# A modulation row stored earlier on VectorE, and the last unit's products and turns in another order, in a two-layer transformer with a Strassen-like MLP

## The reference, cut to what matters

```python
def squared_relu_mlp(h, w_up, w_down):                 # w_up 1024x4096, w_down 4096x1024
    return jnp.square(jax.nn.relu(h @ w_up)) @ w_down
for layer in range(2):
    h = h + mixer(rmsnorm(h, ...))                     # layer 0: recurrence + attention, layer 1: "cd"
    h = h + memory_cross_attention(rmsnorm(h, ...), mem, ...)
    h = h + squared_relu_mlp(rmsnorm(h, mlp_norm[layer]), mlp_w_up[layer], mlp_w_down[layer])
x = rmsnorm(h, final_norm)
mod = jax.nn.silu(c) @ w_ada + b_ada                   # 6 * 1024 numbers, for the second block
x = x + gate1 * hybrid_mixer(rmsnorm(x) * (1 + scale1) + shift1, ...)
x = x + gate2 * expert_choice_ffn(rmsnorm(x) * (1 + scale2) + shift2, ...)
```

## Time and profile before

| what | value |
| --- | --- |
| time, median of 3 runs | 1793.9 us (1791.47 to 1796.63) |
| time of the profiled execution | 1789.16 us |
| its span, first to last instruction | 1787.4 us |
| TensorE busy / weight loads busy | 1545.1 us (86%) / 1140.7 us (64%) |
| VectorE busy / ScalarE busy | 582.3 us (33%) / 260.1 us (15%) |
| mean granted TensorE clock | 0.936 of full speed |

### The profile page before, as it was taken

The page is one execution under the profiler, slowest core; times in us unless marked ns, Lnnn a source line. Parts: engine busy times, 40 slices in busy tenths (PEclk is TensorE's granted clock), DMA queues, the critical chain, the costliest instruction groups (busy, mean ns, idle before and its releaser), DMA issues.

```text
span 1787.4 us, 20576 instructions
## 1 busy us (share of the span) xinstructions
PE 1545.1 (86%) x8896; PEld 1140.7 (64%) x8896; DVE 582.3 (33%) x1259; ACT 260.1 (15%) x610; POOL 30.2 (2%) x52
## 2 busy tenths in 40 slices
PE   6999999999998999999899899989977666655665
PEld 4868688887876777788788788768863222121211
DVE  3633015355633420243556646642330000000000
ACT  1332021000011520210000222222020000000000
POOL 0000000000010000000000002000000000000000
PEclk9999999999999999999999899998979987888877
DMA  9325316664433054157644101432739999999997
GB/s 391 143 94 188 142 48 235 235 253 171 177 141 142 1 192 166 44 210 283 259 147 146 48 1 66 135 107 96 298 126 417 429 429 429 429 429 430 427 429 313
DMA packets 42826, 395.27 MB, mean 221 GB/s; under 512 B 15856, under 2 KB 18288, under 8 KB 19056
## 3 DMA queue, kind: packets, MB, share of 16 engines
q1 hardware_dynamic: 42032, 392.46, 55.4%
q0 software_dynamic: 272, 1.05, 0.2%
q10 hardware_dynamic: 432, 0.44, 0.1%
HBM read 391.31 MB, written 2.62 MB: 220 GB/s over the span
## 4 chain that ended last, share of the span: by engine, by line
PE 72%; DMA 22%; DVE 3%; issue 1%; ACT 1%; ACTq 0%; DVEq 0%
PE pb L445 53%; DMA ring<-in_w_experts 22%; PE pb L836 11%; PE pb L533 6%; DMA small_w<-in_small_w 1%; ACT arena L1315 1%; PE pb L594 1%; PE pb L654 0%; PE pb L1141 0%; DVE arena L1936 0%; DVE hT L1936 0%; DVE rstd L1668 0%; PE pb L1148 0%; PE pb L1001 0%; DVE xT L1915 0%
## 5 line engine op out<-in xcount | busy, mean ns | idle before, releaser
L445 PE MATMUL pb<-hT,ring 128*128 128x256 f32 x2176 | 484.2, 383 | 1.4 <-issue 1.4
L445 PEld LDWEIGHTS pb<-hT,ring 128*128 128x128 f32 x2176 | 413.0, 191 | 64.9 <-issue 9.7
L1315 ACT ACTIVATE arena<-pb 128x512 f32<-128x512 f32 (+4 forms) x166 | 77.9, 480 | 519.5 <-PE pb L445 427.6
L2286 DVE SCALAR_TENSOR_TENSOR side<-side,pb 128x256 f32<-128x256 f32 x16 | 6.7, 421 | 411.6 <-ACT side L1315 411.6
L445 PE MATMUL pb<-ring,hT 128*32 128x512 f32 (+2 forms) x512 | 91.3, 634 | 36.7 <-DMA ring<-in_w_experts 36.7
L533 PE MATMUL pb<-arena,ring 128*128 128x256 f32 x512 | 118.2, 382 | 0.0
L445 PE MATMUL pb<-arena 128*64 128x128 f32 (+5 forms) x592 | 90.4, 420 | 28.5 <-DMA arena<-in_w_experts 16.0
L445 PE MATMUL pb<-ring,arena 128*32 128x512 f32 (+1 forms) x416 | 68.3, 770 | 49.6 <-DMA ring<-in_w_experts 49.6
L533 PEld LDWEIGHTS pb<-arena,ring 128*128 128x128 f32 x512 | 94.9, 190 | 14.6 <-issue 2.9
L445 PEld LDWEIGHTS pb<-arena 128*64 128x64 f32 (+3 forms) x592 | 53.9, 159 | 62.8 <-issue 26.9
L445 PEld LDWEIGHTS pb<-ring,hT 128*32 128x32 f32 (+1 forms) x512 | 32.3, 139 | 84.7 <-DMA ring<-in_w_experts 45.3
(11 more groups left out here) (297 smaller groups left out, 1705.8 us busy)
## 6 DMA issues: line engine op xcount, KB each, us to landing
ring<-in_w_dense SPq DMA_DIRECT2D x86, 2048.0 KB, 8.2
ring<-in_w_experts SPq DMA_DIRECT2D x72, 2048.0 KB, 36.3
arena<-in_w_experts SPq DMA_DIRECT2D x24, 2048.0 KB, 35.9
ring<-in_w_dense SPq DMA_DIRECT2D x2, 1536.0 KB, 6.4
cons<-in_cons SPq DMA_DIRECT2D x1, 1808.0 KB, 19.6
xT<-in_xT SPq DMA_DIRECT2D x1, 1024.0 KB, 6.2
side<-in_memT POOLq DMA_DIRECT2D x1, 1024.0 KB, 6.5
out<-xT SPq DMA_DIRECT2D x4, 256.0 KB, 2.2
```

The lines of the kernel that those rows point to most:

```text
L445: return nc.tensor.matmul(o, l, r, start=st, stop=sp)
L1315: return nc.scalar.activation(o, i, f, **kw)
L2286: V.scalar_tensor_tensor(tg[:, e % 2, :], tg[:, e % 2, :], 1.0, ps[:, 0:S], ALU.add, ALU.mult).then_inc(eg_ready, 1)
```

## The change

Four edits. VectorE stores modulation row 4 ahead of the sums of unit 0, and row 5 between the sums of unit 0 and of unit 1; before, both came behind the sums of units 0 and 1. In the last unit of each half TensorE issues product 1, which needs no sums, last. Product 1 now accumulates in block (3,1) and no longer in (0,1), so that `collect` needs product 5 for five of its instructions and product 1 for the last two, and ScalarE's copy waits for product 0 alone. And features 2 and 3 of each half are turned ahead of 0 and 1; the residual of half 1 is added in the order of chunks 6, 7, 4, 5 (`FINISHED`), and the consumers follow that order.

```diff
+        FINISHED = (0, 1, 2, 3, 6, 7, 4, 5)
@@ TensorE, columns / raw_columns
-                        for k in range(kc):
+                        for i, k in enumerate(order or range(kc)):
...
-                columns(tag, raw, ready=lambda k: pe.wait_ge(raw_ready, base + k + 1), middle=norm_tag)
+                columns(tag, raw, ready=lambda i: pe.wait_ge(raw_ready, base + i + 1), middle=norm_tag,
+                        order=FINISHED if norm_tag == "cd" else None)
@@ TensorE, mlp
-                    for n, (j, l, r, needs) in enumerate((((0, 0), "11", "11", 0), ((0, 1), "12", "21", 0), ...
+                    products = (((0, 0), "11", "11", 0), ((3, 1), "12", "21", 0), ((1, 1), "s1", "t1", 2),
+                                ((2, 0), "s2", "t2", 4), ((1, 0), "22", "t4", 5), ((2, 1), "s3", "t3", 7), ((3, 0), "s4", "22", 8))
+                    order = (0, 2, 3, 4, 5, 6, 1) if g == 3 else range(7)
+                    for n in order:
...
-                        for f in range(4):
+                        for f in (2, 3, 0, 1):
...
-                                pe.wait_ge(q_ready, 8 * layer + 4 * (i == 7) + (1, 2, 4, 3)[2 * (f // 2) + t])
+                                pe.wait_ge(q_ready, 8 * layer + 4 * (i == 7) + (4, 1, 3, 2)[2 * (f // 2) + t])
@@ ScalarE, mlp
-                    ps, _ = full(act, f"pq{layer}_{i}_0")
+                    b, m = product_done[layer, 4 * i + 3, 0]
+                    act.wait_ge(filled[b], m)
+                    ps = pb[:, b, :]
@@ VectorE, mlp
+                modulated(6 * layer + 4)
                 prepare(layer, 0)
+                modulated(6 * layer + 5)
                 prepare(layer, 1)
-                modulated(6 * layer + 4)
-                modulated(6 * layer + 5)
...
-                for c in range(DC):
-                    if c == 4:
+                for at, c in enumerate(FINISHED):
+                    if at == 4:
                         prepare(layer, 7)
                         collect(layer, 1)
@@ VectorE, collect
                 link(V.tensor_tensor(c12, c11, ps[2][:, FEAT[0]], ALU.add))
-                V.tensor_tensor(c11, c11, ps[0][:, FEAT[1]], ALU.add).then_inc(q_ready, 1)
                 link(V.tensor_tensor(c22, c12, ps[2][:, FEAT[1]], ALU.add))
                 link(V.tensor_tensor(c12, c12, ps[1][:, FEAT[1]], ALU.add))
                 V.tensor_tensor(c21, c22, ps[1][:, FEAT[0]], ALU.subtract).then_inc(q_ready, 1)
                 V.tensor_tensor(c22, c22, ps[1][:, FEAT[1]], ALU.add).then_inc(q_ready, 1)
-                product(6)
+                product(1)
                 V.tensor_tensor(c12, c12, ps[3][:, FEAT[0]], ALU.add).then_inc(q_ready, 1)
+                V.tensor_tensor(c11, c11, ps[3][:, FEAT[1]], ALU.add).then_inc(q_ready, 1)
```

More of the change, by code:

```diff
@@ L451, in chunk_wait, with columns @@
                 return lambda k: pe.wait_ge(signal, base + k + 1)
-            def columns(tag, rhs, kc=DC, ready=None, middle=None, banks=(None, None)):
+            def columns(tag, rhs, kc=DC, ready=None, middle=None, banks=(None, None), order=None):
                 w, u = take()
@@ L459, in columns @@
                     for j in range(2):
-                        for k in range(kc):
+                        for i, k in enumerate(order or range(kc)):
                             if ready is not None and b == 0 and j == 0:
-                                ready(k)
+                                ready(i)
                             last = mm(ps[:, j * S:(j + 1) * S], w[:, k, (b + j) * P:(b + j + 1) * P],
-                                      rhs(k) if callable(rhs) else rhs[:, k, :], k == 0, k == kc - 1)
+                                      rhs(k) if callable(rhs) else rhs[:, k, :], i == 0, i == kc - 1)
                     mark(last, f"{tag}{b // 2}", u=u if b + 2 >= nt else None)
@@ L827, in mlp @@
                     step = 8 * (8 * layer + i)
-                    for n, (j, l, r, needs) in enumerate((((0, 0), "11", "11", 0), ((0, 1), "12", "21", 0), ((1, 1), "s1", "t1", 2),
-                                                          ((2, 0), "s2", "t2", 4), ((1, 0), "22", "t4", 5), ((2, 1), "s3", "t3", 7),
-                                                          ((3, 0), "s4", "22", 8))):
+                    products = (((0, 0), "11", "11", 0), ((3, 1), "12", "21", 0), ((1, 1), "s1", "t1", 2),
+                                ((2, 0), "s2", "t2", 4), ((1, 0), "22", "t4", 5), ((2, 1), "s3", "t3", 7), ((3, 0), "s4", "22", 8))
+                    order = (0, 2, 3, 4, 5, 6, 1) if g == 3 else range(7)
+                    for n in order:
+                        j, l, r, needs = products[n]
                         if needs:
@@ L836, in mlp @@
                             last = nc.tensor.matmul(pq[j[0]][:, FEAT[j[1]]], rows_[l](k), cols_[r](k),
-                                                    start=g == 0 and k == 0 and n in (0, 2, 3, 6), stop=g == 3 and k == 3,
+                                                    start=g == 0 and k == 0 and n < 4, stop=g == 3 and k == 3,
                                                     skip_group_check=True)
-                        if n >= 2 or (n == 1 and g == 3):
-                            mark(last, f"pq{layer}_{side_}_{j[0]}", g == 3, u if n == 6 else None)
+                        if n >= 2 or g == 3:
+                            mark(last, f"pq{layer}_{side_}_{j[0]}", g == 3, u if n == order[-1] else None)
                             product_done[layer, i, n] = (pq_bank := fillings[f"pq{layer}_{side_}_{j[0]}"][0], marks[pq_bank])
@@ L899, in _ @@
             pe.wait_ge(norm_sq, 8 * NORMS.index("final") + 16)
-            mm(sums[1][:, 0:S], ones, raw(7), False, False)
-            mark(mm(sums[1][:, 0:S], epsm, sq[:, 7, :], False, True), "norm_n1")
-            mark(mm(sums[0][:, 0:S], ones, sq[:, 7, :], False, True), "norm_final")
+            mm(sums[1][:, 0:S], ones, raw(FINISHED[7]), False, False)
+            mark(mm(sums[1][:, 0:S], epsm, sq[:, FINISHED[7], :], False, True), "norm_n1")
+            mark(mm(sums[0][:, 0:S], ones, sq[:, FINISHED[7], :], False, True), "norm_final")
             ready = chunk_wait(h_ready)
@@ L1493, in mlp @@
                         copied(act, *(f"dn{layer}_0_{f}" for f in range(4)))
-                    ps, _ = full(act, f"pq{layer}_{i}_0")
+                    b, m = product_done[layer, 4 * i + 3, 0]
+                    act.wait_ge(filled[b], m)
+                    ps = pb[:, b, :]
                     fn(quarters[0], ps[:, FEAT[0]], ACT.Copy).then_inc(q_copied, 1)
-                    for c in range(4 * i, 4 * i + 4):
+                    for c in FINISHED[4 * i:4 * i + 4]:
                         copied(act, f"dn{layer}_{c // 4}_{c % 4}")
@@ L1918, in mlp @@
                         V.tensor_scalar(raw(c), xT[:, c, :], gain(c), None, ALU.mult).then_inc(raw_ready, 1)
[L1919 to L1922, removed]
+                        if at > 1:
+                            add_square(at - 1)
+                    elif at > 1:
+                        add_both(at - 1)
             def prepare(layer, i):
@@ L1979, in collect, with add_both, add_square @@
                 V.tensor_tensor(c22, c22, ps[1][:, FEAT[1]], ALU.add).then_inc(q_ready, 1)
-                product(6)
+                product(1)
                 V.tensor_tensor(c12, c12, ps[3][:, FEAT[0]], ALU.add).then_inc(q_ready, 1)
+                V.tensor_tensor(c11, c11, ps[3][:, FEAT[1]], ALU.add).then_inc(q_ready, 1)
                 for j, b in enumerate(banks):
                     V.memset(spare[:, j:j + 1], 0.0).then_inc(freed[b], 1)
-            def add_both(c):
-                dve.wait_ge(norm_sq, 8 * NORMS.index("final") + 2 * c + 2)
+            def add_both(at):
+                c = FINISHED[at]
+                dve.wait_ge(norm_sq, 8 * NORMS.index("final") + 2 * at + 2)
                 for first_, other in ((sq[:, 0, :], sq[:, c, :]), (raw(0), raw(c))):
                     ins = V.tensor_tensor(first_, first_, other, ALU.add)
-                    if c < DC - 2:
+                    if at < DC - 2:
                         link(ins)
-                if c == DC - 2:
+                if at == DC - 2:
                     ins.then_inc(sum_ready, 1)
-            def add_square(c):
-                dve.wait_ge(norm_sq, 8 * NORMS.index("cd") + c + 1)
+            def add_square(at):
+                c = FINISHED[at]
+                dve.wait_ge(norm_sq, 8 * NORMS.index("cd") + at + 1)
                 ins = V.tensor_tensor(sq[:, 0, :], sq[:, 0, :], sq[:, c, :], ALU.add)
-                if c < DC - 1:
+                if at < DC - 1:
                     link(ins)
```

## The result

The changed kernel takes 1783.95 us (median of 11 runs, 1777.14 to 1789.76) against 1794.18 us (11 runs, 1791.47 to 1797.28). The ratio over all these runs is 0.9935, with a 95% interval of 0.9919 to 0.9951: 11.7 us faster, between 8.8 and 14.5 (the two medians alone lie 10.2 us apart). The forecast was 12.3 us. The profiled execution took 1778.01 us with a span of 1776.2, 11.2 us shorter than the span before.

The account below looks back on a forecast made before the run. TensorE bounds the kernel (72% of the chain), idling 4.06 us per layer behind a late VectorE store, then running at half clock. Terms: 13.7 - 1.4 = 12.3 us, median 1793.9 to 1781.6 us; range 1777.7 to 1787.

Parts of the forecast that it names:

- Part 1: Down stages, behind unit 0: earlier stores free bank 4, removing TensorE's pause and half-speed stretch; gain 13.7 us over both layers.
- The cover of the new wait: Unit 1: products 0 and 1 hide VectorE's wait for row 5; smallest margin 1.3 us, otherwise about 2 us lost per layer.
- Part 2: Last unit of each half: product 1 last lets collecting start earlier; gain 0.04 us, called nothing.
- Part 3: Layer 0, `cd_qc0`: bank 0 is freed only by the third addition, so TensorE pauses 2.2 us; loss 1.4 us.
- A: At `cd_qc0`: no wait on bank 0, as some other wait hides it; 1780.2 us, chance 0.08.
- C: Unit 1: VectorE's strict queue holds the sums back beyond the margin, 2 us or more a layer; 1785.6 us, chance 0.04.
- Rival B: Clock stays low behind unit 0, or half-speed stretches at other, shifted pauses eat the gain; 1787.5 to 1789.5 us, chance 0.12.
- Rival D: Rest of the program: half-speed stretches elsewhere make the kernel slower, ten giving 1801.6 us; chance 0.02.

Follow-up runs that it names:

- e1: Kernel before with only the two modulation stores moved ahead, orders of products, turns and additions unchanged; ratio 0.9915 to the kernel before.
- e7: Changed kernel with row 5 stored behind the sums of unit 1, row 4 still ahead of unit 0's sums; ratio 0.9925 to the kernel before.
- e4: Kernel before with 16 unread matmul instructions in the pause ahead of row 5, in both layers; ratio 0.9925 to the kernel before.
- e6: Changed kernel with 10 unread matmul instructions in the pause ahead of `cd_qc0`, layer 0; ratio 0.9908 to the kernel before.
- e2: Changed kernel with the two modulation stores put back behind the sums of units 0 and 1, new orders kept; ratio 1.0023 to the kernel before.
- e9: Changed kernel with 8 unread matmul instructions at the start of each MLP; ratio 0.9904 to the kernel before.
- e11: Changed kernel run once more, unaltered; ratio 0.9941 to the kernel before.
- e3: Changed kernel with `cd_qc0` in bank 2, of the chunk added first, and `cd_qc1` in bank 0; ratio 0.9911 to the kernel before.
- e8: Changed kernel with `cd_qc0` in bank 2, plus 16 and 10 unread matmul instructions in two pauses ending layer 1; ratio 0.9874 to the kernel before.
- e10: Kernel before with both stores moved, plus unread matmul instructions: 8 starting each MLP, 16 and 10 ending layer 1; ratio 0.9885 to the kernel before.

## Why the prediction was right

**Part 1, the modulation.** The forecast was 6.87 and 6.8 us, the measured gain is 7.02 and 6.98 (e1). The reading of the cause, bank 4 held by row 4's store, is shown by e7. The split was forecast as some 4 us of pause and 2.9 of clock; e4 gives 4.3 and 2.7. Row 5's matmuls to the first product took 0.81 us (404.18 to 404.99) and not 1.05, and row 4's store moved the sums by 0.07 us and not 0.15. The cover of the new wait held with 1.25 us. One reading was loose: row 4's store stood behind eighteen sums and not ten, nine for each of units 0 and 1. Nothing in the sum hangs on it.

**Part 2, product 1 last.** The forecast was 0.04 us, the measured gain is 0.07 (e1 against changed), which can't be told from nothing. It is worth nothing because it only trades: five of seven `collect` instructions go under the products, but VectorE then waits for a product that ends 1.7 us later.

**Part 3, the order of the additions.** The mechanism, place and layer were right: bank 0, freed by the third addition, in layer 0 alone, with a forecast pause of 2.2 us and a measured one of 2.26. The wait was sized well, 1.4 us against 1.47 (e6). The clock behind it was not: I took 0, with 2 us as a bound, and it is 1.68 us, so the loss is 3.15 us. Judging this pause by its predecessors of 0.44 and 0.48 us, a fifth as long, was the weak step. In all five traces in which `cd_qc0` waits unfilled (changed, e2, e7, e9, e11), its first 16 instructions take 5.2 us: so here the clock fell every time. The pauses of 2 us at the start of the MLPs, which I had weighed against it, end both ways, as the earlier trace rows shows; what sets this one apart (eight short turns stand ahead of it) no run tests.

**The sum.** 13.7 - 1.4 = 12.3 forecast; 14.0 - 3.1 = 10.9 by the stretches, 11.2 by the spans, 11.7 by the ratio. The ratio lies nearer to the forecast than the stretches do, and that is luck: the terms were off by +0.3 and -1.7 us, and the interval of the ratio is 5.7 us wide. Rivals A and C are out by e3 and e7. Rival B is out for units 1 to 5, and B's other half, the clock at pauses whose moment shifted, goes with the +2.25 and -1.69 us outside the change, which nearly cancel. Rival D did not happen. The strict first-in first-out queue that the Trainium skill ("TensorE: Matmul & The Clock Gate", table at its head) gives VectorE agrees with the trace: the nine sums of unit 1 stood behind one waiting store for 4.39 us (forecast 4.7). It cost nothing.

## What to carry to other kernels

Where an engine waits for a PSUM bank, look for the small, long-ready store that holds it, and move that store ahead of the long work on its engine. When the order in which results are drained is changed, follow the banks in order as well: the next user should take the bank that is freed first. And price a pause of TensorE with the clock behind it: here a delay of 4.3 us cost 7.0 and one of 1.5 us cost 3.1.

## What the runs showed of the hardware

A pause of TensorE that is filled with matmuls nobody reads keeps the granted clock at 1.00 (e4, e6, e8), and the time behind it gets shorter by 1.7 to 2.9 us although not one wait is removed. It is no cure for all: in e8 the clock fell later, in a stretch where the profile shows TensorE busy throughout, and e10 lost the tail's gain again.

I had not expected that a handful of such instructions, placed hundreds of microseconds ahead, would also take some 5 us from a stretch of small matmuls near 1200 us: 35.4 to 37.3 us without them, 30.5 to 32.3 with them. There TensorE pauses between instructions that have no semaphore, and each of the 18 pauses ends 1.2 to 1.5 us behind the landing of a 16,384-byte packet of instructions. This makes the time of an experiment with added or removed TensorE instructions hard to read: e4's time alone would have been taken for a clock gain of 13.5 us, where the stretches show 5.4.
